# Threading attention through projections: logits first in a beat, another spread of the pieces, value differences later

## The chip, the cores and the metric

The kernel runs on one core of a Trainium2 chip. The metric is the device time of one execution in microseconds; the time before is the median of three runs. The core's engines are named as the profile names them: PE (matmuls and transposes), DVE (elementwise work, scans, reductions), ACT (activation functions, copies, scaling), POOL (masks, some transfers), SP (the queue of most transfers). PEld is PE's loading of weights into its array.

## The reference, cut to what matters

Two transformer blocks follow each other over 512 tokens of width 1024, in fp32.

```
h    = rmsnorm(concat(meta[16], x)) ; proj = h @ w_in
# block 1: eight "forgetting" heads beside a pooled path
s    = q.k / 8 + c[t] - c[s]   (causal; c is the running sum of log gates) ; p = softmax(s)
y    = (p @ v) * silu(z_attn)
x    = rmsnorm(x + merge(pooled path, y) @ w_out)
# block 2: eight heads with relative position bias, eight "stick-breaking" heads, MLP
p_ca = softmax(q.k / 8 + bias[rel], within chunks)
w_sb = exp(log_sigmoid(z) + suffix sum of log_sigmoid(-z))      (strictly causal)
x    = x + gt1 * (concat(w_sb @ v, p_ca @ v) @ w_o)
x    = x + gt2 * (relu(h2 @ w1)**2 @ w2)
```

Each head is 64 wide; queries are taken in four blocks of 128 rows.

## The kernel before

**Precision.** Every operand of a large product is kept as an upper part and a lower part of a rounded format (`hh` and `hl`, `wh` and `wl`, `ah` and `al`, `pth` and `ptl`), and a product is three matmuls (upper x upper, lower x upper, upper x lower; L1842 to L1844). The upper part is a copy on ACT, the lower a subtraction on DVE.

**Projections and steps.** The weights are cut into 76 units of 128 x 2048, loaded by SP into `raw`, copied to `wh` by ACT (L582) and subtracted to `wl` by DVE (L1081) in four parts of 128 x 512. Two such pairs exist, so a unit's parts are made while PE works on the unit before. PE walks through a unit in 16 steps of three matmuls with 512 columns each; the upper and lower parts of queries, keys and values that come out are made on ACT and DVE at fixed steps (L695, L706, L1228, L1239).

**Attention in pieces.** Attention is not a stage of its own. It is cut into pieces, and after each projection step PE issues as many pieces as a list of numbers says. `pieces_of` writes the row of pieces, `beats_of` spreads it. A piece is one of three:
- S h.i: the scores of head h, query block i, with keys 0 to i (L1988). Blocks go 3, 2, 1, 0.
- T h.j: transposes ("turns") of the probabilities of key block j, one for each query block from j on (L2009), into PSUM bank 3 or 6 in turn. A turn waits until DVE has emptied the bank of the turn before the last one.
- V h.j: values of key block j times the turned probabilities (L2038, L2041).

The row has the turns of head h and the scores of head h + 1 in alternation, then the values of head h. Heads 0 to 7 (called FG) run beside 160 steps of the first block, heads 8 to 15 (CA) and 16 to 23 (SB) beside 188 steps of the second. A place in the list is a beat; it holds one piece, or none if the head's queries and keys aren't ready at that step.

**The other engines** go through the same beats in the same steps, each task so many beats behind its piece (the table `AGE`). For an S on DVE: logits (L1253 with the row of sums, L1261 with the position bias) one beat behind, the maximum (L1268) two, the reciprocal (L1273) four, or, for heads 16 to 23, a scan (L1282) two. On ACT: the exponential (L714) three, the product with the reciprocal (L720, `norm`) five, or the sigmoid (L726) one. For a T: upper part on ACT one (`ph`, L739), lower part on DVE two (`pl`, L1293; the text calls its result ptl). For a head's last V: half of the output on ACT (L745), `both_out` on DVE (L1301), the gate (L1306), upper and lower part of the output (L754, L1311). Engines execute their instructions in the order written, so in a beat the order of tasks is the order in the queue.

**Value differences.** The value rows of the second block go to memory and come back shifted by one row (L523, L533). DVE subtracts them at the four steps in `DV` (L1576), ACT makes the upper part a step later (`DV_UPPER`, L974), DVE the lower part one step after that (`DV_LOWER`, L1580). The value pieces of heads 16 to 23 read them.

Of the kernel before, what the change touches and what calls it, by code (L numbers as in the profile page):

```python
# [55 lines left out]
FG, CA, SB = range(8), range(8, 16), range(16, 24)  # L56
# [13 lines left out]
def pieces_of(heads):  # L70

    out = []
    for n, h in enumerate([*heads, None]):
        scores = [] if h is None else [("S", h, i) for i in (3, 2, 1, 0)]
        if n:
            g = heads[n - 1]
            blocks = range(3, LAST_J[g] - 1, -1)
            for j in blocks:
                out.append(("T", g, j))
                if scores:  # L80
                    out.append(scores.pop(0))
            out += [("V", g, j) for j in blocks]
        for x in scores:
            out += [x] if n else [x, None]
    return out

AGE = dict(logits=1, max=2, exp=3, rcp=4, norm=5, sig=1, scan=2, ph=1, pl=2, half=1, both=2, oh=3, ol=4,
           gate=3, oh_fg=4, ol_fg=5)  # L90


def beats_of(pieces, per_step, ready):

    flat, first = [], []
    for g, n in enumerate(per_step):
        first.append(len(flat))
        for _ in range(n):
            flat.append(pieces.pop(0) if pieces and ready(pieces[0]) <= g else None)
    first.append(len(flat))  # L100
    return flat + pieces + [None] * 12, first


def program(nc, x, xcols, wall, wf, poolw, params, fng, wada, crow_in, rel, out):
# [30 lines left out]
    with ExitStack() as ctx:  # L135
        def sb(name, shape, dt=F32, where=ctx):
            return where.enter_context(nc.sbuf_tensor(name, shape, dt))
# [34 lines left out]
        half = sb("half", [128, 16])  # L172
# [111 lines left out]
        def raw_of(n, c):  # L284
# [2 lines left out]

        steps_f = 16 * 10
        f_qk = {p: m for m, (kind, p) in enumerate(ORDER_1) if kind == "qk"}
        beats_f, first_f = beats_of(pieces_of(FG), [0] * 16 + [1] * 112 + [1, 2] * 16,  # L290
                                    lambda x: 0 if x is None else 16 * (f_qk[x[1] // 2] + 1) + 7)

        steps_s = 188
        beats_s, first_s = beats_of(
            pieces_of(CA) + pieces_of(SB), [1, 1, 1, 1, 2] * 22 + [1, 1] + [1, 2] * 24 + [2] * 7 + [4] * 5 + [1] * 16,
            lambda x: 0 if x is None else 16 * (x[1] // 2 - 4) + 33 if x[1] in CA else 16 * (x[1] // 2 - 8 + 7) + 9 - 2 * (x[1] > 21))
        end_f, end_s = len(beats_f), len(beats_s)

# [70 lines left out]
        def ends(x):  # L369
            return x is not None and x[0] == "V" and x[2] == LAST_J[x[1]]  # L370
# [35 lines left out]
        TURN_BANK_2 = ((1, 0), (4, 5))  # L406
        VSB_OUT = (78, 79, 91, 95)

        DV, DV_UPPER, DV_LOWER = (87, 88, 104, 108), (88, 89, 105, 109), (89, 90, 106, 110)
        VSB_BANK, W_O_BANK = (0, 1, 2, 0), ((1, 0, 4, 5), (2, 3, 6, 7))  # L410

        def o_step(n):
# [159 lines left out]
        def _(e):  # L572
# [183 lines left out]
            def beat(flat, b_):  # L756
                def at(age):
                    return flat[b_ - age] if b_ >= age else None

                if (x_ := at(AGE["norm"])) and x_[0] == "S" and x_[1] not in SB:  # L760
                    normalize(*x_[1:])
                if ends(x_ := at(AGE["oh_fg"])) and x_[1] in FG and x_[1] % 2:
                    out_upper(x_[1])
                if ends(x_ := at(AGE["oh"])) and x_[1] not in FG and x_[1] % 2:
                    out_upper(x_[1])
                if (x_ := at(AGE["exp"])) and x_[0] == "S" and x_[1] not in SB:
                    exp(*x_[1:])
                if (x_ := at(AGE["sig"])) and x_[0] == "S" and x_[1] in SB:
                    sigmoid(*x_[1:])
                if (x_ := at(AGE["ph"])) and x_[0] == "T":  # L770
                    turned(*x_[1:])
# [305 lines left out]
        def _(e):  # L1077
# [236 lines left out]
            def beat(flat, b_):  # L1314
                def at(age):
                    return flat[b_ - age] if b_ >= age else None

                if ends(x_ := at(AGE["ol_fg"])) and x_[1] in FG and x_[1] % 2:
                    out_lower(x_[1])
                if ends(x_ := at(AGE["ol"])) and x_[1] not in FG and x_[1] % 2:  # L1320
                    out_lower(x_[1])
                if (x_ := at(AGE["rcp"])) and x_[0] == "S" and x_[1] not in SB:
                    inverse_sum(*x_[1:])
                if (x_ := at(AGE["scan"])) and x_[0] == "S" and x_[1] in SB:
                    sticks(*x_[1:])
                if ends(x_ := at(AGE["gate"])) and x_[1] in FG and x_[1] % 2:
                    out_gate(x_[1])
                if (x_ := at(AGE["max"])) and x_[0] == "S" and x_[1] in FG:
                    maximum(*x_[1:])
                if (x_ := at(AGE["pl"])) and x_[0] == "T":  # L1330
                    turned(*x_[1:])
                if ends(x_ := at(AGE["both"])):
                    both_out(x_[1])
                if (x_ := at(AGE["logits"])) and x_[0] == "S" and x_[1] not in SB:
                    logits(*x_[1:])


            e.wait_ge(a["v"], 5)
# [59 lines left out]
            for b_ in range(first_f[steps_f], end_f):  # L1398
                beat(beats_f, b_)
# [1010 lines left out]
```

## Time and profile before

| | |
|---|---|
| median of three runs | 1009.93 us (1009.12 to 1011.12) |
| profiled execution | 1012.43 us |
| its span | 1010.6 us |
| PE, PEld busy | 980.9 us (97%), 817.1 us (81%) |
| DVE, ACT busy | 657.3 us (65%), 485.5 us (48%) |

The profile is of one execution, whose time is a little above the median. The span is the time from the first to the last recorded instruction; 1.8 us of the execution's time lie outside it. Busy times are sums over an engine's instructions, and matmuls overlap, so a busy PE is not PE at its peak. A row of a timeline gives a start, a duration and, in brackets, how long the engine was idle before it and which instruction's end released it.

### The profile page before, as it was taken

Reading aid. Unit: us, or ns where it says so; the run is one execution under the profiler, and the core shown is the slowest. Engines: PE = TensorE matmul, PEld = TensorE weight load, DVE = VectorE, ACT = ScalarE, POOL = GpSimd, SP = SyncE. Lnnn points to the kernel's source line nnn. Section 1 sums busy time; section 2 is a strip of 40 time slices with the busy share of each in tenths; the row PEclk is TensorE's granted clock in tenths of the full one; section 3 lists DMA queues with packets and bytes.
Section 4 is the critical chain, followed back from the end, with each engine's and each line's share of the span. In section 5 each row is a group of like instructions: output and inputs, shape, how many; then the busy total and the mean of one; then the engine's idle time right before and its main releaser. Section 6 shows DMA issues by size and latency. Waiting matters only on the chain.

```text
span 1010.6 us, 13022 instructions
## 1 busy us (share of the span) xinstructions
PE 980.9 (97%) x4784; PEld 817.1 (81%) x4784; DVE 657.3 (65%) x1203; ACT 485.5 (48%) x963; POOL 70.5 (7%) x158
## 2 busy tenths in 40 slices
PE   8999999999999999999889999899999999999998
PEld 7888988788888888777778778788888888888886
DVE  6487878859787768467577776877444454445453
ACT  6458687743223445589685654334124223323420
POOL 4001001011112011000000000110000000000000
PEclk9999999999999999999999999999999999999999
DMA  7104221257789415342433225337413223322221
GB/s 294 75 25 178 67 103 53 84 197 291 286 289 331 174 56 153 114 125 78 136 94 115 63 63 207 127 103 131 163 56 112 84 86 123 107 102 84 84 73 52
DMA packets 34080, 129.81 MB, mean 128 GB/s; under 512 B 8905, under 2 KB 8905, under 8 KB 24418
## 3 DMA queue, kind: packets, MB, share of 16 engines
q1 hardware_dynamic: 23538, 98.27, 29.0%
q0 software_dynamic: 7408, 26.75, 7.6%
q10 hardware_dynamic: 3072, 3.98, 1.1%
q8 instruction: 38, 0.62, 0.3%
q14 instruction: 24, 0.20, 0.1%
HBM read 119.45 MB, written 5.27 MB: 123 GB/s over the span
## 4 chain that ended last, share of the span: by engine, by line
PE 78%; DVE 12%; ACT 4%; issue 3%; DMA 2%; SPq 0%; POOL 0%; ACTq 0%; DVEq 0%; POOLq 0%
PE psum L1842 23%; PE psum L1844 23%; PE psum L1843 23%; PE psum L2009 2%; DVE wl L1081 2%; PE psum L1988 2%; PE psum L2038 1%; PE psum L2041 1%; DMA raw<-in_wall 1%; DVE two L1620 1%; DVE ptl L1293 1%; DVE p_sb L1282 1%; DMA value_rows<-rows 1%; DVE hl L1121 1%; DVE tmp L1599 1%
## 5 line engine op out<-in xcount | busy, mean ns | idle before, releaser
L1842 PE MATMUL psum<-hh,wh 128*128 128x512 f32 (+1 forms) x720 | 277.2, 385 | 0.7 <-DVE hl L1121 0.6
L1844 PE MATMUL psum<-hh,wl 128*128 128x512 f32 (+1 forms) x720 | 268.5, 373 | 0.0
L1843 PE MATMUL psum<-hl,wh 128*128 128x512 f32 (+1 forms) x720 | 268.2, 373 | 0.0
L582 ACT ACTIVATE wh<-raw 128x512 fp32r<-128x512 f32 x292 | 169.5, 620 | 134.9 <-PE psum L1844 118.9
L1081 DVE TENSOR_TENSOR wl<-raw,wh 128x512 fp32r<-128x512 f32 x292 | 192.5, 684 | 18.1 <-ACT wh L582 17.6
L1844 PEld LDWEIGHTS psum<-hh,wl 128*128 128x128 f32 x720 | 135.6, 188 | 24.1
L1842 PEld LDWEIGHTS psum<-hh,wh 128*128 128x128 f32 x720 | 135.8, 189 | 22.8 <-DVE hl L1121 1.6
L1843 PEld LDWEIGHTS psum<-hl,wh 128*128 128x128 f32 x720 | 136.0, 189 | 19.1 <-issue 0.7
L1842 PE MATMUL psum<-wh,ah 128*128 128x512 f32 x320 | 125.8, 393 | 0.0
L1844 PE MATMUL psum<-wh,al 128*128 128x512 f32 x320 | 124.6, 389 | 0.0
L1843 PE MATMUL psum<-wl,ah 128*128 128x512 f32 x320 | 124.6, 389 | 0.0
L1599 DVE TENSOR_TENSOR tmp<-psum,gt 128x512 f32<-128x512 f32 x40 | 27.6, 690 | 86.3 <-PE psum L1844 85.5
L1844 PEld LDWEIGHTS psum<-wh,al 128*128 128x128 f32 x320 | 60.1, 188 | 12.6
L1842 PEld LDWEIGHTS psum<-wh,ah 128*128 128x128 f32 x320 | 60.1, 188 | 12.1 <-ACT p_sb L726 0.2
L1843 PEld LDWEIGHTS psum<-wl,ah 128*128 128x128 f32 x320 | 60.1, 188 | 11.7
L1682 DVE SCALAR_TENSOR_TENSOR sgt<-psum,two 128x512 f32<-128x512 f32 x32 | 22.1, 691 | 61.3 <-ACT two L1036 61.3
L2009 PE MATMUL psum<-ident,p_sb 128*128 128x128 f32 x272 | 48.5, 281 | 12.1 <-DVE ptl L1293 11.9
L1036 ACT ACTIVATE two<-psum 128x512 f32<-128x512 f32 x32 | 19.2, 600 | 78.4 <-PE psum L1844 78.4
L739 ACT ACTIVATE pth<-psum 128x128 fp32r<-128x128 f32 (+4 forms) x104 | 46.1, 445 | 21.8 <-PE psum L2009 21.1
L2009 PEld LDWEIGHTS psum<-ident,p_sb 128*128 128x128 f32 x272 | 34.7, 144 | 24.7 <-issue 16.2
L1293 DVE TENSOR_TENSOR ptl<-psum,pth 128x128 fp32r<-128x128 f32 (+1 forms) x96 | 46.2, 482 | 10.5 <-ACT pth L739 9.8
L714 ACT ACTIVATE p_sb<-p_sb,sm 128x528 f32<-128x528 f32 (+3 forms) x64 | 35.9, 561 | 8.6 <-DVE sm L1268 5.6
(282 smaller groups left out, 1468.0 us busy)
## 6 DMA issues: line engine op xcount, KB each, us to landing
raw<-in_wall SPq DMA_DIRECT2D x75, 1024.0 KB, 5.0
wa<-in_wada POOLq DMA_DIRECT2D x20, 512.0 KB, 5.9
gt<-in_wada POOLq DMA_DIRECT2D x20, 512.0 KB, 7.1
wb<-in_wada POOLq DMA_DIRECT2D x8, 512.0 KB, 7.3
xt<-in_xcols SPq DMA_DIRECT2D x8, 264.0 KB, 8.4
cb<-c_rows SPq DMA_DIRECT2D x8, 264.0 KB, 3.5
x<-in_x SPq DMA_DIRECT2D x4, 512.0 KB, 8.1
x_kept<-x SPq DMA_DIRECT2D x4, 512.0 KB, 2.8
```

Source lines behind the costliest of these rows:

```text
L582: e.activation(home(w)[0][:, 512 * c:512 * c + 512], raw_of(w, c), ACT.Copy).then_inc(a["wh"], 1)
L714: e.activation(block_p(h, i), block_p(h, i), ACT.Exp, bias=nmx, scale=1.0 if h in FG else -1.0, accum_out=su).then_inc(a["exp"], 1)
L739: e.activation(ph[0:rows, PT[j]:PT[j] + w_], bank[bk][0:rows, 0:w_], ACT.Copy).then_inc(a["turn"], 1)
L1081: e.tensor_tensor(home(w)[1][:, cs], raw_of(w, c), home(w)[0][:, cs].bitcast(F32), ALU.subtract).then_inc(v["wl"], 1)
L1293: e.tensor_tensor(dst, bank[bk][0:rows, 0:w_], ph[0:rows, o:o + w_].bitcast(F32), ALU.subtract).then_inc(v["turn"], 1)
L1599: e.tensor_tensor(dst, bank[bk], gt[:, j, 512 * ch:512 * ch + 512], ALU.mult).then_inc(sem, 1)
L1682: e.scalar_tensor_tensor(s2[n % 2], bank[w1_bank(n)], 0.0, two[:, n % 2, :], ALU.max, ALU.mult).then_inc(v["r2"], 1)
L1842: e.matmul(out_, lh, rh, start=start, stop=False, skip_group_check=True)
L1843: e.matmul(out_, lh, rl, start=False, stop=False, skip_group_check=True)
L1844: return e.matmul(out_, ll, rh, start=False, stop=stop, skip_group_check=True)
L1988: ins = e.matmul(dst[:, size * j:size * j + size], q[:, 128 * i:128 * i + 128], k[:, size * j:size * j + size], start=k is k_up, stop=k is ...
L2009: ins = e.transpose(bank[bk][:, 128 * (i - i0):128 * (i - i0) + 128], head(h)[0][:, o:o + 128], ident[:, :])
```

## The change

Four things are changed, and no instruction is added or taken away.

- `logits` is the first task of a DVE beat instead of the last.
- `AGE["norm"]` is 6 instead of 5.
- The numbers of pieces for each step come from two tables of digits, `PACE_F` and `PACE_S`, instead of regular lists. The old lists had one piece a step or a little more; the new ones have steps without a piece and steps with up to nine. Their sums are the same, 160 and 256.
- `DV`, `DV_UPPER` and `DV_LOWER` have the differences of row blocks 2 and 3 at steps 113 and 122 (and one and two steps later) instead of 104 and 108. Those of row blocks 0 and 1 stay at 87 and 88.

```diff
+PACE_F = [int(n) for n in ("00000000000000000011140110040102202010113010211101010115131000301121010101301202"
...
+PACE_S = [int(n) for n in ("11112111121111211112111121111211112002211200322014011101112010312102222120002304"
...
-AGE = dict(logits=1, max=2, exp=3, rcp=4, norm=5, sig=1, scan=2, ph=1, pl=2, half=1, both=2, oh=3, ol=4,
+AGE = dict(logits=1, max=2, exp=3, rcp=4, norm=6, sig=1, scan=2, ph=1, pl=2, half=1, both=2, oh=3, ol=4,
            gate=3, oh_fg=4, ol_fg=5)
...
-        beats_f, first_f = beats_of(pieces_of(FG), [0] * 16 + [1] * 112 + [1, 2] * 16,
+        beats_f, first_f = beats_of(pieces_of(FG), PACE_F,
...
-            pieces_of(CA) + pieces_of(SB), [1, 1, 1, 1, 2] * 22 + [1, 1] + [1, 2] * 24 + [2] * 7 + [4] * 5 + [1] * 16,
+            pieces_of(CA) + pieces_of(SB), PACE_S,
...
-        DV, DV_UPPER, DV_LOWER = (87, 88, 104, 108), (88, 89, 105, 109), (89, 90, 106, 110)
+        DV, DV_UPPER, DV_LOWER = (87, 88, 113, 122), (88, 89, 114, 123), (89, 90, 115, 124)
...
+                if (x_ := at(AGE["logits"])) and x_[0] == "S" and x_[1] not in SB:
+                    logits(*x_[1:])
                 if ends(x_ := at(AGE["ol_fg"])) and x_[1] in FG and x_[1] % 2:
                     out_lower(x_[1])
...
                 if ends(x_ := at(AGE["both"])):
                     both_out(x_[1])
-                if (x_ := at(AGE["logits"])) and x_[0] == "S" and x_[1] not in SB:
-                    logits(*x_[1:])
```

Line numbers of the changed kernel are 7 higher. The order of instructions at three places follows, first of the kernel before, then of the changed one.

DVE at the start of head 5 (p_sb is written by the logits, tmp 64x512 by both_out, tmp<-tmp,gt is the gate, ptl the turned lower part), before:

```order
L1301 TENSOR_TENSOR tmp<-psum,tmp 64x512
L1081 TENSOR_TENSOR wl<-raw,wh 128x512
L1228 SCALAR_TENSOR_TENSOR ah<-psum,ah 64x512 x2
L1306 TENSOR_TENSOR tmp<-tmp,gt 128x512
L1293 TENSOR_TENSOR ptl<-psum,pth 128x128
L1253 SCALAR_TENSOR_TENSOR p_sb<-psum,ccol,cb 128x528
```

The same place after:

```order
L1088 TENSOR_TENSOR wl<-raw,wh 128x512
L1235 SCALAR_TENSOR_TENSOR ah<-psum,ah 64x512 x2
L1308 TENSOR_TENSOR tmp<-psum,tmp 64x512
L1260 SCALAR_TENSOR_TENSOR p_sb<-psum,ccol,cb 128x528
L1313 TENSOR_TENSOR tmp<-tmp,gt 128x512
L1300 TENSOR_TENSOR ptl<-psum,pth 128x128
```

The logits of the head's first block have moved ahead of the gate and of the turned lower part.

DVE around the turns of head 14 and 15 (ptl2 is the turned lower part, sgt<-sgt,rows the difference of value row block 3, v_sb<-sgt,v_sb its lower part, x1<-x1,v_end the difference of row block 2, sm a reciprocal), before:

```order
L1273 RECIPROCAL sm<-sm 128x1
L1576 TENSOR_TENSOR sgt<-sgt,rows 128x512
L1081 TENSOR_TENSOR wl<-raw,wh 128x512
L1273 RECIPROCAL sm<-sm 128x1
L1301 TENSOR_TENSOR tmp<-psum,tmp 64x512
L1580 TENSOR_TENSOR v_sb<-sgt,v_sb 128x8x64
L1081 TENSOR_TENSOR wl<-raw,wh 128x512
L1293 TENSOR_TENSOR ptl2<-psum,pth2 128x128
L1293 TENSOR_TENSOR ptl2<-psum,pth2 128x256
L1293 TENSOR_TENSOR ptl2<-psum,pth2 128x384
```

The same place after:

```order
L1280 RECIPROCAL sm<-sm 128x1
L1088 TENSOR_TENSOR wl<-raw,wh 128x512 x2
L1308 TENSOR_TENSOR tmp<-psum,tmp 64x512
L1300 TENSOR_TENSOR ptl2<-psum,pth2 128x128
L1300 TENSOR_TENSOR ptl2<-psum,pth2 128x256
L1583 TENSOR_TENSOR x1<-x1,v_end 128x512
L1246 TENSOR_TENSOR low_2<-psum,k_sb2 64x512
L1300 TENSOR_TENSOR ptl2<-psum,pth2 128x384
```

The difference and its lower part have left the place ahead of the first ptl; that of row block 2, which stood earlier, now stands between the second ptl and the third.

DVE at head 18 (128x512 of p_sb2 is the scan of head 19's first block, low_2 a lower part of keys, al the output's lower part), before:

```order
L1301 TENSOR_TENSOR tmp<-psum,tmp 64x512
L1293 TENSOR_TENSOR ptl2<-psum,pth2 128x128
L1239 TENSOR_TENSOR low_2<-psum,k_sb2 64x512
L1311 TENSOR_TENSOR al<-tmp,ah 128x512
L1282 SCALAR_TENSOR_TENSOR p_sb2<-p_sb2,rows 128x512
L1239 TENSOR_TENSOR low_2<-psum,k_sb2 64x512
L1293 TENSOR_TENSOR ptl2<-psum,pth2 128x256
```

The same place after:

```order
L1246 TENSOR_TENSOR low_2<-psum,k_sb2 64x512 x2
L1308 TENSOR_TENSOR tmp<-psum,tmp 64x512
L1300 TENSOR_TENSOR ptl2<-psum,pth2 128x128
L1318 TENSOR_TENSOR al<-tmp,ah 128x512
L1289 SCALAR_TENSOR_TENSOR p_sb2<-p_sb2,rows 128x512
L1300 TENSOR_TENSOR ptl2<-psum,pth2 128x256
```

Both lower parts of keys stand ahead of the head's first ptl, and none is left between the scan and the second ptl.

## Rows read from the trace of the kernel before

**Rows 1.** The page's busy time, share of the span and instructions, by engine.

```profile
PE 980.9 (97%) x4784; PEld 817.1 (81%) x4784; DVE 657.3 (65%) x1203; ACT 485.5 (48%) x963; POOL 70.5 (7%) x158
```

**Rows 2.** Windows: length, then PE, PEld, DVE, ACT, POOL busy (x), PEclk, DMA, GB/s.

```profile
80.00:212.00 132.00, 127.09 (x804) 112.91 (x803) 106.37 (x219) 99.06 (x218) 13.26 (x33) 0.99 0.26 86
430.00:535.00 105.00, 95.09 (x464) 76.91 (x464) 69.76 (x187) 84.57 (x197) 2.80 (x12) 0.97 0.39 116
535.00:625.00 90.00, 85.80 (x464) 71.00 (x463) 67.57 (x111) 50.82 (x109) 2.19 (x4) 1.00 0.26 81
665.00:1010.60 345.60, 341.69 (x1527) 283.29 (x1526) 170.77 (x267) 103.78 (x184) 2.74 (x5) 1.00 0.31 99
```

**Rows 3.** Windows of 6 us behind PE's two longest waits.

```profile
504.00:510.00 6.00, 4.88 (x20) 4.34 (x21) 5.58 (x17) 5.57 (x14) 0.00 (x0) 0.72 0.20 45
528.00:534.00 6.00, 5.55 (x24) 4.78 (x25) 3.16 (x7) 2.83 (x5) 0.00 (x0) 0.72 0.73 223
```

**Rows 4.** PE's waits, 430 to 535: who waited <- for whom: total us, times, longest.

```profile
PE psum L2009 <- DVE ptl L1293: 6.1, 3, 2.6
PE psum L1988 <- DMA low<-low: 1.2, 1, 1.2
PE psum L1842 <- DVE wl L1081: 1.1, 1, 1.1
PE psum L1842 <- DVE qk L1557: 0.8, 1, 0.8
PE psum L2271 <- ACT two L959: 0.6, 1, 0.6
```

**Rows 5.** PE's waits, 535 to 625.

```profile
PE psum L2009 <- DVE ptl L1293: 3.9, 4, 1.3
PE psum L2038 <- DVE ptl L1293: 0.2, 1, 0.2
```

**Rows 6.** PE's timeline, heads 0 to 7: start, us, instruction, [idle before <- releaser].

```profile
94.28 0.64 PE L1988 MATMUL psum<-k_sb,ah 128*128 128x400 f32 x2 [1.30 <-DVE p_sb L1253]
...
154.57 0.63 PE L1988 MATMUL psum<-k_sb,ah 128*128 128x400 f32 x2 [1.57 <-DVE p_sb L1253]
...
200.24 0.93 PE L2009 MATMUL psum<-ident,p_sb 128*128 128x128 f32 x4 [1.93 <-DVE ptl L1293]
```

**Rows 7.** DVE's timeline, value differences of row block 0, then 3.

```profile
499.25 0.69 DVE L1576 TENSOR_TENSOR x<-x,rows 128x512 f32<-128x512 f32 x1 [3.61 <-DMA x<-value_rows]
...
523.78 0.67 DVE L1576 TENSOR_TENSOR sgt<-sgt,rows 128x512 f32<-128x512 f32 x1
...
526.82 0.67 DVE L1580 TENSOR_TENSOR v_sb<-sgt,v_sb 128x512 fp32r<-128x512 f32 x1
```

**Rows 8.** DVE's timeline at head 18.

```profile
568.12 1.21 DVE L1282 TENSOR_TENSOR_SCAN p_sb<-p_sb,rows 128x512 f32<-128x512 f32 x1
569.35 0.69 DVE L1239 TENSOR_TENSOR low<-psum,k_sb 64x512 fp32r<-64x512 f32 x1
570.08 0.43 DVE L1293 TENSOR_TENSOR ptl<-psum,pth 128x256 fp32r<-128x256 f32 x1
```

**Rows 9.** DVE's timeline at the start of head 5.

```profile
152.83 0.69 DVE L1306 TENSOR_TENSOR tmp<-tmp,gt 128x512 f32<-128x512 f32 x1
153.55 0.29 DVE L1293 TENSOR_TENSOR ptl<-psum,pth 128x128 fp32r<-128x128 f32 x1
153.76 0.76 DVE L1253 SCALAR_TENSOR_TENSOR p_sb<-psum,ccol,cb 128x528 f32<-128x528 f32 x1
```

**Rows 10.** PE's timeline, turns of heads 13, 15 and 18, and a score.

```profile
505.12 0.71 PE L2009 MATMUL psum<-ident,p_sb 128*128 128x128 f32 x3 [2.63 <-DVE ptl L1293]
...
528.45 0.52 PE L2009 MATMUL psum<-ident,p_sb 128*128 128x128 f32 x3 [2.58 <-DVE ptl L1293]
...
565.80 0.63 PE L1988 MATMUL psum<-v_ca 128*128 128x512 f32 x2
...
570.65 0.52 PE L2009 MATMUL psum<-ident,p_sb 128*128 128x128 f32 x3 [0.97 <-DVE ptl L1293]
```

More of the change, by code:

```diff
@@ L85, in pieces_of @@
     return out
-AGE = dict(logits=1, max=2, exp=3, rcp=4, norm=5, sig=1, scan=2, ph=1, pl=2, half=1, both=2, oh=3, ol=4,
+PACE_F = [int(n) for n in ("00000000000000000011140110040102202010113010211101010115131000301121010101301202"
+                           "02000112030230300100300103023301100000110301311112112203021301123113200500330023")]
+PACE_S = [int(n) for n in ("11112111121111211112111121111211112002211200322014011101112010312102222120002304"
+                           "10211203011201010231200160011001211203331201110233120022213230100115031020203441"
+                           "3020305539041021021210001211")]
+AGE = dict(logits=1, max=2, exp=3, rcp=4, norm=6, sig=1, scan=2, ph=1, pl=2, half=1, both=2, oh=3, ol=4,
            gate=3, oh_fg=4, ol_fg=5)
```

## The prediction, on record before the result

> **What bounds the kernel now.** I read the page's busy line first. PE is busy 980.9 of 1010.6 us [rows 1], so about 30 us can be won on TensorE at all, and DVE and ACT matter only where PE waits for them. The windows then say where those 30 us lie. The change touches only the stretches in which attention is threaded through projections: 80 to 212 us (heads 0 to 7), 430 to 535 (heads 8 to 15) and 535 to 625 (heads 16 to 23). PE is idle there 132.00 − 127.09 = 4.9, 105.00 − 95.09 = 9.9 and 90.00 − 85.80 = 4.2 us, 19.0 together [rows 2].
>
> A long wait costs a second time. Over the three stretches the granted clock reads 0.99, 0.97 and 1.00 [rows 2], but it reads 0.72 in the 6 us from 504 and in the 6 us from 528 [rows 3], just behind the two longest waits: 6 × (1 − 0.72) = 1.7 us of lost work each, in which PE still reads busy. The ceiling is 19.0 + 3.4 = 22.4 us.
>
> The Trainium skill ("Perfetto Trace Analysis", Identifying the Most-Contended Engine) says that the busy share of matmuls is a poor measure, since they are pipelined, and that the weight loads' share is a good one. The trace agrees at the low clock, where PE reads 5.55 of 6 us busy [rows 3]. By that rule 430 to 535 (76.91 of 105 us) would lose 105 × (1 − 0.732 / 0.820) = 11.3 us against the undisturbed end of the program (283.29 of 345.60) [rows 2], where idle time gives 9.9. My sum would be about a seventh larger by it, which lies inside its uncertainty.
>
> Who ends the waits? In 430 to 535 three waits for the lower part of turned probabilities (DVE L1293) make 6.1 us; the rest is a DMA of keys 1.2, a weight's lower half 1.1, a normalised query 0.8, and squares from ACT 0.6 [rows 4]. In 535 to 625 it is L1293 again, 3.9 in four waits [rows 5]. In the first stretch the three longest are two waits for logits (1.30, 1.57) and one for L1293 (1.93) [rows 6]. L1293 itself is short, 0.29 to 0.43 us [rows 8, 9]: what is late is what stands ahead of it in DVE's and ACT's queues.
>
> **Part one, logits first.** DVE does the same instructions in another order. At head 5's start the gated product (0.69) and a ptl (0.29) stand ahead of the logits at 153.76 [rows 9], for which PE waits 1.57 at 154.57 [rows 6]. In the new order they stand behind, so the logits end 0.98 earlier, and PE comes to the waiting score one projection step later. A step is three matmuls, and where nothing disturbs them 1527 take 345.60 us [rows 2], 0.23 each: a step is 0.70. 0.98 + 0.70 covers 1.57: **+1.6**. The wait of 1.30 at 94.28 is of the same kind, but there a weight's lower half comes to stand ahead of the logits: I take half, **+0.7** (0 to 1.3). The price of logits first is that each ptl of the beat waits one logits (0.76 [rows 9]) more. In the old order the beat before had put the same logits ahead of it, so this shows only at the first turned block of a head, and nobody waits for that one alone.
>
> **Part two, normalising a beat later.** The product on ACT goes one beat behind, so ACT's queue no longer stops for a reciprocal just made. Who waits for it is the turn that reads it. In the order of pieces ten or more stand between a score and that turn, against an age of six: no cost, and if a bunch eats the cover, a product (under 0.76, the logits' time for the same block [rows 9]). The exceptions are heads 0 and 8, where six stand. At T8.0 the product and a turned upper part share a beat on an ACT that is busy 84.57 of 105 us [rows 2]: I take a new wait of 0.9 (0 to 1.3), charged below.
>
> **Part three, the spread of pieces.** The totals are the same, so PE's own work is. SP's queue moves one load of a head's row of sums past one load of a weight unit, POOL's keeps its order; no wait of PE is for either load [rows 4 to 6], so both cost 0. What changes is which wait falls where.
> - 200.24 (1.93 [rows 6]) moves to the next turn, a quarter of a step on: **+0.3**.
> - 430 to 500: the DMA wait of 1.2 stays, since the first score of head 8 waits for its keys, ahead of all pieces. The other four (6.1 less the two of 2.63 and 2.58 leaves 0.9; then 0.6, 0.8, 1.1) [rows 4, 10] are 3.4; steps with no piece come to stand ahead of three of them. I leave 0.5 and charge T8.0's 0.9: 3.4 − 0.5 − 0.9 = **+2.0** (0 to 3.4).
> - T13.1 at 505.12 (2.63 [rows 10]): DVE had stood 3.61 us for rows of values coming back by DMA [rows 7]. Neither that subtraction's step nor the transfer moves. PE now arrives two steps (1.40) sooner, and DVE has a logits (about 0.67) ahead of the ptl where it had a lower half of values and one of weights, 2 × 0.67 by the form at 526.82 [rows 7], so 0.67 less. 2.63 + 1.40 − 0.67 = 3.4, and ACT's copy of values stands behind more: wait 3.6, **−1.0** (0 to −2.7). Its low clock stays.
> - The two longest of 535 to 625, 0.97 at 570.65 (head 18's last turn) [rows 10] and 1.3 (head 20's) [rows 5]: ahead of the ptl that the first waits for, DVE does a scan (1.21), then a lower half of keys (0.69) [rows 8]. In the new order both lower halves of keys (1.38) come before the scan, where DVE waits anyway. That is more than the step (0.70) by which the distance on PE shrinks. **+1.0** and **+1.3**. The other two waits of the stretch stay: 0. The 0.2 for a value piece [rows 5] goes, **+0.2**.
>
> **Part four, value differences later.** The difference of row block 3 (0.67) and its lower half (0.67) stand on DVE at 523.78 and 526.82 [rows 7], ahead of the ptl for which PE waits 2.58 at 528.45 [rows 10]. They go to steps 122 and 124, with ACT's copy between them; those of row block 2 come to steps 113 and 115, behind the second ptl of the head, where no wait is. They move past lower halves of weights and keys and head 15's pieces; their readers are the value pieces of head 16, over ten steps behind, so they cost nothing there (without that cover, 0.67 each). With 1.34 less on DVE about 0.6 of the wait is left: 2.0. With a wait that short the clock should not fall, since it did not behind 0.97 and 1.3 (1.00 over 535 to 625 [rows 2, 5]): 1.7. **+3.7**.
>
> **New waits.** Bunches are new. In step 104 six pieces stand together, and the third (T14.0) takes over a PSUM bank whose ptl stands behind a logits: 0.67 + 0.43 on DVE against about 0.6 for two pieces on PE, so 0.5. In step 147 five pieces stand together, with a scan of 1.21 [rows 8] ahead of a ptl. No row prices these; the nearest are the short waits of [rows 4, 5], 0.2 to 1.1. I take five places at 0.56, nearest to the one worked out: **−2.8** (0 to −6).
>
> Sum: 1.6 + 0.7 + 0.3 + 2.0 − 1.0 + 1.0 + 1.3 + 0.2 + 3.7 = 9.8; less 2.8 is 7.0. The profiled execution took 1012.43 us (span 1010.6 and 1.8 around it), 0.25% above the median of the runs: 1005.4 is 0.69% less, so 1009.93 becomes **1003.0**.
>
> **Rivals.**
> - *Smaller gain.* ACT, 81% busy in 430 to 535 [rows 2], sets the pace: part three's +2.0 is 0, T13.1 costs 2.0 rather than 1.0, and the terms of 535 to 625 are halved (−1.2). 9.8 − 4.2 − 2.8 = 2.8, median 1007.1. Against it: of the waits of [rows 4] one is named for ACT, 0.6.
> - *Slower: the latency stays.* From the score at 565.80 to the turn at 570.65 pass 4.85 us [rows 10]. If the chain of sigmoid, scan and both turned parts takes that whatever stands beside it, a bunch only takes a step (0.70) out of PE's distance, and each joint between heads pays: heads 16 to 19 two steps at four joints, 5.6; heads 8 to 13 one step at five, 3.5; head 15 one, 0.7; 9.8 together. Of the gains are left 1.6 + 0.7 + 0.3 + 1.0 (half of +2.0) + 0.2 + 1.7 (the clock at 528) = 5.5. Net 4.3 slower, median 1014.2. It decides where DVE has less than 0.7 us of movable work ahead of the ptl. Against it: at 569.35 such work, 0.69, is seen inside the chain [rows 8].
> - *Everything on L1293 and the logits goes*: 1.3 + 1.57 + 1.93 + 6.1 + 3.9 + 0.2 = 15.0, and one low clock, 1.7: 16.7, median 993.3. The 3.61 us for value rows speak against it.
> - *No change:* the new waits are as large as the 9.8, median 1009.9. That the pieces don't move at all is excluded by the order of instructions.
>
> **How the numbers follow.** Forecast 0.48 (its own range 1000 to 1006), smaller gain 0.25, slower 0.14, all gone 0.07, no change 0.06. A measurement can tell about 0.2%, 2.0 us, from no change: faster is below 1007.9, slower above 1011.9. The smaller gain lies a third of the time within the bound: faster 0.48 + 0.17 + 0.07 = 0.72, same 0.08 + 0.06 = 0.14, slower 0.14. The range 997.5 to 1010.0 leaves out the slower case and most of the one in which all goes.
>
> **What would show it.** Right: the wait of head 5's score gone; no wait over 1 us near 528 and a clock of 1.00 there; PE idle in 535 to 625 near 2; DVE still waiting 3 to 4 us for value rows, with a PE wait of about 3.6 and a low clock behind it. Wrong: waits for L1293 of over 1 us inside the bunches of steps 104 and 147, or a clock of 0.72 at a place that had none; then the allowance is what failed.

## The result, and the profile after

The changed kernel takes 994.56 us (median of four runs, 993.92 to 996.30) against 1009.60 of the kernel before: a ratio of 0.985, with a 95% interval of 0.9836 to 0.9863. The prediction had 1003.0 and a range from 997.5 to 1010.0. The direction was right, the gain was twice what was forecast, and the time lies below the range.

The profiled execution of the changed kernel has a span of 992.8 us, 17.8 less than the 1010.6 of before. The medians differ by 15.0: the execution that was profiled before was one of the slower ones. The page's busy line (engine, busy us, share, instructions), to be read against [rows 1]:

```profile
PE 974.2 (98%) x4784; PEld 813.3 (82%) x4784; DVE 656.1 (66%) x1203; ACT 483.6 (49%) x963; POOL 69.9 (7%) x158
```

The same instructions, and DVE and ACT as busy as before. PE's busy time fell by 6.7 us although its work is the same.

To see where 17.8 us went, a stage has to be cut at the same matmul in both kernels, not at the same time. I cut at the first matmuls of five weight units: heads 0 to 7 run from 75.21 to 216.71 before and from 74.90 to 211.75 after; heads 8 to 15 from 418.74 to 534.90 and from 413.82 to 520.22; heads 16 to 23 from 534.90 to 656.24 and from 520.22 to 638.45. Outside these the two differ by 0.3 us. Windows of the kernel before, cut so (columns as in [rows 2]):

```profile
75.21:216.71 141.50, 136.47 (x851) 120.76 (x849) 114.27 (x232) 105.06 (x228) 14.76 (x36) 0.99 0.28 92
418.74:534.90 116.16, 106.25 (x510) 85.26 (x508) 76.50 (x197) 91.74 (x210) 2.80 (x12) 0.97 0.39 116
534.90:656.24 121.34, 114.41 (x601) 94.47 (x600) 96.24 (x167) 63.94 (x138) 4.81 (x10) 1.00 0.32 110
```

And of the changed kernel:

```profile
74.90:211.75 136.85, 134.49 (x851) 119.29 (x849) 111.50 (x229) 103.04 (x226) 12.62 (x33) 1.00 0.28 94
413.82:520.22 106.40, 101.86 (x507) 81.94 (x506) 74.48 (x195) 90.44 (x209) 2.80 (x12) 1.00 0.42 127
520.22:638.45 118.23, 113.96 (x603) 94.87 (x603) 98.03 (x171) 64.11 (x139) 4.82 (x10) 1.00 0.33 113
```

The stages are 4.65, 9.76 and 3.11 us shorter. The second column gives PE's idle time as length less busy: 5.0, 9.9 and 6.9 before, 2.4, 4.5 and 4.3 after, so 10.7 us of idle time went. The seventh column is the granted clock: 0.99 and 0.97 became 1.00. Before, there were three falls of the clock in these stages (near 200, 505 and 528 us), after there is none. A window of 6 us around one reads 0.72; windows of 3.4 us inside each (columns as above) show what a fall is:

```profile
201.50:204.90 3.40, 3.40 (x13) 2.74 (x12) 3.37 (x6) 1.90 (x4) 0.00 (x0) 0.50 0.00 0
505.30:508.70 3.40, 3.40 (x14) 3.02 (x13) 3.26 (x11) 2.97 (x8) 0.00 (x0) 0.50 0.34 77
529.20:532.60 3.40, 3.40 (x13) 2.82 (x13) 1.70 (x3) 2.63 (x5) 0.00 (x0) 0.50 0.84 291
```

For 3.4 us the clock is 0.50 (1.2 GHz, the lower of its two levels) and then 1.00 again, which costs half of 3.4, 1.7 us; three falls are 5.1 us. What is left, 17.5 − 10.7 − 5.1 = 1.7 us, is neither idle time nor clock; it comes up again below.

PE's waits in the stage of heads 8 to 15 after, to be read against [rows 4] (who waited <- for whom: total us, times, longest):

```profile
PE psum L2016 <- DVE ptl L1300: 2.7, 2, 2.2
PE psum L1849 <- DVE wl L1088: 1.2, 2, 0.7
PE psum L1995 <- DMA low<-low: 0.5, 1, 0.5
```

The 6.1 us in three waits for the turned lower part are 2.7 in two, and the waits for a query and for squares are gone.

### The profile page after: what moved, and what is told of

Its sections match the earlier page's. It is cut to its first block, busy times and chain, and to the rows that moved or that the text cites. A ratio compares the mean times of both kernels' runs of the same rounds, so it can differ in the third digit from the quotient of the medians.

```text
span 992.8 us, 13022 instructions
## 1 busy us (share of the span) xinstructions
PE 974.2 (98%) x4784; PEld 813.3 (82%) x4784; DVE 656.1 (66%) x1203; ACT 483.6 (49%) x963; POOL 69.9 (7%) x158
## 4 chain that ended last, share of the span: by engine, by line
PE 82%; DVE 9%; ACT 4%; issue 2%; DMA 2%; POOL 0%; SPq 0%; DVEq 0%; ACTq 0%; POOLq 0%
PE psum L1849 24%; PE psum L1851 24%; PE psum L1850 24%; PE psum L2016 2%; PE psum L1995 2%; PE psum L2045 1%; PE psum L2048 1%; DVE wl L1088 1%; DVE two L1627 1%; PE psum L1883 1%; DVE hl L1128 1%; DMA value_rows<-rows 1%; ACT wh L589 1%; DVE two L1492 1%; DMA raw<-in_wall 1%
## 5 line engine op out<-in xcount | busy, mean ns | idle before, releaser
L1849 PE MATMUL psum<-hh,wh 128*128 128x512 f32 (+1 forms) x720 | 274.0, 381 | 0.7 <-DVE hl L1128 0.6
```

Source lines behind the costliest of these rows:

```text
L1849: e.matmul(out_, lh, rh, start=start, stop=False, skip_group_check=True)
```

## The experiments

Each kernel is timed against the kernel before on the same chip. The table at the end of this section gives the three stages of each from its profile. Two theories stood against each other. Theory A: the new spread of the pieces brings most. Theory B: the order of tasks within DVE's and ACT's queues brings most.

**Logits first alone** moves the two lines of `logits` to the head of a DVE beat:

```diff
+                if (x_ := at(AGE["logits"])) and x_[0] == "S" and x_[1] not in SB:
+                    logits(*x_[1:])
                 if ends(x_ := at(AGE["ol_fg"])) and x_[1] in FG and x_[1] % 2:
                     out_lower(x_[1])
...
-                if (x_ := at(AGE["logits"])) and x_[0] == "S" and x_[1] not in SB:
-                    logits(*x_[1:])
```

> The kernel before with logits first in each DVE beat and nothing else. Theory A (the spread of pieces brings most of the 15 us): only the two waits for logits in heads 0 to 7 get shorter (1.57 and 1.30), 1 to 2.5 us faster, nothing in heads 8 to 23. Theory B (the order within DVE's and ACT's queues brings most): about 5 us faster, with the waits for L1293 in heads 8 to 15 shorter too. On record my prediction had +1.6 for head 5 alone.

Measured: a ratio of 0.9999 (0.9987 to 1.0011), no change. The two waits for logits shrank from 2.9 us to 1.3, and the stage of heads 0 to 7 lost 1.2 us of idle time. But heads 8 to 15 gave it back: T13.1 waited 3.65 us instead of 2.63, and T10.1 1.42 instead of 0.85; the stage has 0.6 us more idle time. Part of the 1.0 at T13.1 is the new order: its ptl now stands behind a logits of 0.68, and from the first value difference to that ptl pass 5.71 us instead of 5.45. The larger part is that PE stood at the turn 2.5 us after the value rows were there, and not 3.2. Why that distance shrank is not shown. Both theories had expected a gain.

**The product one beat later alone** (`norm=5` to `norm=6`):

> The kernel before with ACT's product with the reciprocal one beat later and nothing else. Theory A: within 1 us of before. Theory B: ACT no longer stops for reciprocals, about 3 us faster, most of it between 430 and 535 us.

Measured: 0.9959 (0.9941 to 0.9977), 4 us faster. PE's waits between 418 and 530 us in its profile:

```profile
PE psum L2016 <- DVE ptl L1300: 3.9, 3, 1.8
PE psum L1849 <- DVE wl L1088: 1.1, 1, 1.1
PE psum L1849 <- DVE qk L1564: 0.8, 1, 0.8
PE psum L1995 <- DMA low<-low: 0.5, 1, 0.5
```

The 6.1 of [rows 4] are 3.9, the wait for squares from ACT is gone, and of two falls of the clock one is left. That is theory B's number, for this part. ACT, the busiest engine behind PE in this stage, had been stopping for reciprocals, and turned upper parts and squares were queued behind. Its waits for them in this stage, before and in this kernel:

```profile
ACT p_sb L720 <- DVE sm L1273: 4.4, 9, 0.9
ACT p_sb L727 <- DVE sm L1280: 0.6, 2, 0.4
```

**Value differences later alone** (steps 113 and 122 for blocks 2 and 3):

```diff
-        DV, DV_UPPER, DV_LOWER = (87, 88, 104, 108), (88, 89, 105, 109), (89, 90, 106, 110)
+        DV, DV_UPPER, DV_LOWER = (87, 88, 113, 122), (88, 89, 114, 123), (89, 90, 115, 124)
```

> The kernel before with the differences of value row blocks 2 and 3 at steps 113 and 122 and nothing else. Both theories: the wait of 2.58 us at 528 falls to 0.6 and the low clock of 1.7 us behind it goes, 3 to 4 us faster; the wait at T13.1 (2.63) and its low clock stay. If the low clock does not hang on that wait, 2 us.

Measured: 0.9984 (0.9968 to 1.0001), too small to be clear of no change. In the profile the mechanism is as expected: T15.1's wait fell from 2.58 to 0.76 us, and the low clock behind it went, 3.5 us together. But in the next stage a new wait of 0.61 stands at 543.9, and that stage is 1.2 us longer. The differences are not free at steps 122 to 124: the wait of about 0.6 is in all three profiles with the regular spread and the differences late. The 1.2 is not all theirs, since the kernel before has 122.12 instead of 121.34 in a second profile.

**The spread alone** (both tables, nothing else):

```diff
-        beats_f, first_f = beats_of(pieces_of(FG), [0] * 16 + [1] * 112 + [1, 2] * 16,
+        beats_f, first_f = beats_of(pieces_of(FG), PACE_F,
...
-            pieces_of(CA) + pieces_of(SB), [1, 1, 1, 1, 2] * 22 + [1, 1] + [1, 2] * 24 + [2] * 7 + [4] * 5 + [1] * 16,
+            pieces_of(CA) + pieces_of(SB), PACE_S,
```

> The kernel before with both tables of the spread and nothing else. Theory A: 9 to 12 us faster. Theory B: the spread was made for the other order of tasks and alone brings 0 to 3 us, with waits for logits inside the bunches of over 1 us each.

Measured: 998.78 us, 0.9889 (0.9868 to 0.991), 11.4 us faster: theory A. All three stages are shorter, by 3.2, 7.7 and 3.1 us. Its waits between 415 and 524:

```profile
PE psum L2016 <- DVE ptl L1300: 2.8, 2, 2.6
PE psum L1849 <- DVE wl L1088: 1.1, 2, 0.6
PE psum L1849 <- DVE qk L1564: 0.6, 1, 0.6
PE psum L1995 <- DMA low<-low: 0.5, 1, 0.5
```

The long one is T15.1's, 2.61 us at 518, with a low clock behind it; the value differences are still at steps 104 and 108 here.

**The changed kernel less one part.** Four kernels take one part back each, with the diffs above reversed.

> The changed kernel with logits last in each DVE beat again. Theory A: 1 to 3 us slower than the changed kernel (about 996.5). Theory B: 6 us or more slower (over 1000.5), with PE waits for logits in the bunches.

> The changed kernel with ACT's product at age 5 again. Theory A: within 1 us of the changed kernel, T8.0's wait a little shorter. Theory B: 3 us or more slower, between 430 and 520 us.

> The changed kernel with the value differences of row blocks 2 and 3 at steps 104 and 108 again. They then stand in and behind the bunch of six pieces at step 104. If the value differences were what held T15.1: 3 to 4 us slower with a clock of 0.72 near 516 us. If the spread has already moved T15.1 away from them: within 1 us.

> The changed kernel with the regular spread of before (so logits first, product later and value differences later, together). Theory A: 9 to 11 us slower than the changed kernel, near 1004. Theory B: 3 us slower at most, near 997.

Measured, with the changed kernel at 994.56 us (ratio 0.985):
- logits last: 997.04, 0.9871 (0.9857 to 0.9886). Logits first is worth 2.5 us here (2.1 by the two ratios), where alone it was worth nothing. The difference between the two profiles is mostly in heads 0 to 7 (139.01 against 136.85): waits for logits of 1.0 us come back instead of 0.2, idle time grows by 1.1 us in all, and another 1.1 is neither idle time nor clock.
- product at age 5: 994.07, 0.984 (0.9824 to 0.9856). The part that alone brought 4 us brings nothing beside the others. ACT does stop for reciprocals again, 2.8 us in nine waits in this stage, but with the new spread nobody on PE's path stands behind it.
- value differences early: 997.22, 0.9881 (0.9864 to 0.9897), 2.7 us slower. T15.1's wait is back, without a fall behind it in this profile:

```profile
517.71 0.52 PE L2016 MATMUL psum<-ident,p_sb 128*128 128x128 f32 x3 [2.21 <-DVE ptl L1300]
```

- the old spread: 1006.18, 0.9963 (0.9951 to 0.9974). The three other parts together bring 3.7 us, the spread on top of them 11.6. Theory A, but its 9 to 11 was a little low.

**What holds T13.1.** The prediction said that this wait would grow, because DVE stands for value rows that come back by DMA. In the changed kernel it is 2.19 us. DVE's rows ahead of it, then PE's row:

```profile
490.48 0.69 DVE L1583 TENSOR_TENSOR x<-x,rows 128x512 f32<-128x512 f32 x1 [3.64 <-DMA x<-value_rows]
491.99 0.69 DVE L1583 TENSOR_TENSOR x<-x,rows 128x512 f32<-128x512 f32 x1 [0.81 <-DMA x<-value_rows]
```

```profile
494.82 0.41 PE L2016 MATMUL psum<-ident,p_sb 128*128 128x128 f32 x2 [2.19 <-DVE ptl L1300]
```

DVE's wait of 3.64 is that of [rows 7]. ACT's upper part of the same turn was ready at 492.96, 1.4 us before DVE came to the ptl at 494.40, so ACT doesn't set this turn:

```profile
492.68 0.28 ACT L746 ACTIVATE pth<-psum 128x128 fp32r<-128x128 f32 x1
```

Two kernels put the differences of row blocks 0 and 1 at steps 91 and 93, behind T13.1's tasks, one with the product at age 6 and one at 5:

```diff
-        DV, DV_UPPER, DV_LOWER = (87, 88, 113, 122), (88, 89, 114, 123), (89, 90, 115, 124)
+        DV, DV_UPPER, DV_LOWER = (91, 93, 113, 122), (92, 94, 114, 123), (93, 95, 115, 124)
```

> The changed kernel with the differences of value row blocks 0 and 1 also later, at steps 91 and 93 instead of 87 and 88, behind T13.1 in DVE's order. Theory V (DVE stands for the value rows' transfer, and T13.1 waits for that): the wait of 2.19 us at T13.1 goes, none takes its place, 2 us faster than the changed kernel, near 992.5. Theory W (the turned upper part on ACT sets T13.1): the wait stays within 0.5 us of 2.19 and the time too.

> As the last one, with ACT's product at age 5 as before. If the later product has no worth with the new spread: the same time as the last one, within 0.1%. If it costs something: 1 us faster than it.

Measured: 993.04 (0.9841, 0.981 to 0.9872) and 993.50 (0.9846, 0.9815 to 0.9877). Theory V: the 2.19 is gone. But a wait took part of its place, so the gain was 1.5 us and not 2; with age 6:

```profile
PE psum L1849 <- DVE wl L1088: 1.2, 2, 0.7
PE psum L2045 <- DVE ptl L1300: 0.7, 1, 0.7
PE psum L2016 <- DVE ptl L1300: 0.5, 1, 0.5
PE psum L1995 <- DMA low<-low: 0.5, 1, 0.5
```

The 0.7 at L2045 is a value piece behind block 1's instructions. The age of the product makes no difference that can be told, as before.

**Is the spread needed for the long waits?** The kernel before, with its regular spread and logits last, with age 6 and all four differences late (91, 93, 113, 122):

> The kernel before, regular spread and logits last, with the product one beat later and all four value differences later (91, 93, 113, 122). If the two long waits of heads 13 and 15 hang on the value differences alone, both go with both low clocks, with what the later product brings: about 8 us faster than before, near 1002. If the new spread is needed for them: 1005 or more.

Measured: 1003.32 us, 0.9938 (0.9921 to 0.9955), 6.3 us faster where about 8 was expected. Its stage of heads 8 to 15 is 106.69 us, only 0.3 longer than the changed kernel's 106.40:

```profile
PE psum L1849 <- DVE wl L1088: 1.2, 1, 1.2
PE psum L2016 <- DVE ptl L1300: 1.1, 2, 0.6
PE psum L1849 <- DVE qk L1564: 0.8, 1, 0.8
PE psum L1995 <- DMA low<-low: 0.5, 1, 0.5
```

So in this stage there were two ways to nearly the same gain: to move what stood ahead of two ptl's, or to move PE's pieces. The gains don't add: this kernel is 9.5 us shorter here than the one before, the spread alone 7.7, both together (with logits first, differences at 91 and 93) 11.1. They overlap in T13.1's wait and its fall, which the profile with the spread alone doesn't have either (2.6 + 1.7), in the wait for squares (0.6) and in the DMA wait (1.15 to 0.5 in both). T15.1's wait goes with the value differences only; the spread alone leaves it at 2.61. In the stages of heads 0 to 7 and 16 to 23 this kernel is no shorter than the one before (141.29 against 141.50, 122.72 against 121.34); there the spread is what helps.

**Keys between scan and ptl.** The prediction's +1.0 and +1.3 rested on the lower halves of keys that stand on DVE between a scan and a ptl [rows 8]. This kernel is the one before with those halves two steps later for two groups:

```diff
-                    SB_LOWER.setdefault(n_ + (9 if p_ == 3 and sub_ else 10), []).append((p_, sub_, part_))
+                    SB_LOWER.setdefault(n_ + (11 if p_ == 3 and sub_ else 12 if p_ == 2 and sub_ else 10), []).append((p_, sub_, part_))
```

> The kernel before with the lower halves of head pair 20's and 22's keys two steps later on DVE (148 and 149, 163 and 164 instead of 146, 147 and 161, 162), so that none stands between the scan and the turned lower part. My prediction's theory: the waits of 0.97 at T18.0 and 1.34 at T20.0 go, 2.0 to 2.3 us faster. Rival (the chain of sigmoid and scan sets them, as in the slower case of the prediction): both waits stay above 0.7.

Measured: 1.0036 (1.0019 to 1.0053), 3.6 us slower, and yet the theory holds for the waits. T18.0's 0.97 is gone (0.43 is left at a value piece), T20.0's 1.34 is 0.47. What was missed is the other reader of those instructions. The halves read the PSUM bank into which the next projection writes, and PE came there first (v_ca is here the buffer in which the keys lie):

```profile
593.12 0.78 PE L1842 MATMUL psum<-wh,ah 128*128 128x512 f32 x1 [2.93 <-DVE v_ca L1239]
```

```profile
592.00:598.00 6.00, 4.88 (x19) 4.26 (x20) 2.64 (x5) 0.00 (x0) 0.00 (x0) 0.72 0.19 44
```

A wait of 2.93 us and 1.7 us of low clock, where 1.4 were won (0.97 + 1.34, less the 0.43 and 0.47 that are left). The changed kernel leaves the keys where they are and moves the pieces.

**Does a fall of the clock belong to a wait or to an execution?** Three kernels were profiled a second time: the changed kernel, the one before, and logits first alone.

> The changed kernel, profiled a second time. If a fall of the clock belongs to a wait: again none behind the wait of about 2.2 us at T13.1 near 495, and the stages as long as before to 0.3 us, but for the value rows' transfer. If it belongs to the execution: a clock of 0.72 for 6 us in one place, 1.7 us more.

> The kernel before, profiled a second time. If a fall belongs to a wait: the same three, behind 200, 505 and 528 us, 5.1 us. If to the execution: another number or other places.

> The kernel before with logits first alone, profiled a second time. The same wait of 1.93 us near 200: with a low clock behind it this time if the execution decides, without one if the kernel does.

Both, as it came out. The changed kernel again has no fall (stages 136.67, 106.30, 118.33). The kernel before again has the two in heads 8 to 15, but not the one near 200, although the wait is the same. The window behind the wait in the first execution (its row stands in [rows 6]), then the row of the wait and the window in the second:

```profile
200.00:206.00 6.00, 5.65 (x25) 4.68 (x26) 5.45 (x10) 3.12 (x7) 0.00 (x0) 0.72 0.00 0
```

```profile
200.10 1.14 PE L2009 MATMUL psum<-ident,p_sb 128*128 128x128 f32 x6 [1.93 <-DVE ptl L1293]
```

```profile
200.00:206.00 6.00, 5.80 (x32) 4.56 (x32) 5.36 (x9) 2.99 (x7) 0.00 (x0) 1.00 0.00 0
```

Logits first alone had no fall near 200 in either. Over all profiles with that wait of 1.93 us, six had the fall and three had not. Of eleven waits of 2.48 to 3.94 us in heads 13 and 15 ten had a fall right behind them; the eleventh, 2.83 us in the first profile of logits first, had none, and the fall behind the wait before it lasted twice as long. No wait under 1.7 us in the three stages had one.

**The last wait of that kind.** The changed kernel with block 0's difference at step 91 and block 1's at 98:

```diff
-        DV, DV_UPPER, DV_LOWER = (87, 88, 113, 122), (88, 89, 114, 123), (89, 90, 115, 124)
+        DV, DV_UPPER, DV_LOWER = (91, 98, 113, 122), (92, 99, 114, 123), (93, 100, 115, 124)
```

> The changed kernel with the value difference of row block 0 at step 91 and that of block 1 at step 98. Theory V: the wait of 0.72 at 500 in the run with 91 and 93 was for a ptl behind block 1's instructions and goes, 0.7 us faster than that run, near 992.3. Rival: that wait is for the bunch of value pieces itself and stays; then the same time.

Measured: 992.70 us (992.40 to 992.88), 0.9822 (0.9801 to 0.9843), the fastest version. The wait of 0.7 at L2045 is 0.2:

```profile
PE psum L1849 <- DVE wl L1088: 1.2, 2, 0.7
PE psum L1995 <- DMA low<-low: 0.5, 1, 0.5
PE psum L2016 <- DVE ptl L1300: 0.5, 1, 0.5
PE psum L2045 <- DVE ptl L1300: 0.2, 1, 0.2
```

In the trace the stage is 104.66 us against 105.10; by the medians, 0.34 us between two sessions on two chips, the two kernels can't be told apart. Against the changed kernel its runs lie 1.9 us lower and don't overlap (the highest is 992.88, the lowest of the changed kernel 993.92).

**All stages.** Length in us of the stage, PE's idle time in it, and the number of falls of the clock in it, from one profile each (the two of logits first in its first profile are one of 6.8 us):

```
kernel                              heads 0-7        heads 8-15       heads 16-23
before                              141.50  5.0  1   116.16  9.9  2   121.34  6.9  0
before again                        139.84  5.1  0   115.28  9.1  2   122.12  7.3  0
changed                             136.85  2.4  0   106.40  4.5  0   118.23  4.3  0
changed again                       136.67  2.2  0   106.30  4.4  0   118.33  4.3  0
before + logits first               138.99  3.9  0   115.98 10.5  2   121.40  7.0  0
before + logits first, again        139.16  3.9  0   116.98 10.9  2   121.41  7.0  0
before + product later              141.32  5.1  1   111.46  6.7  1   121.14  6.7  0
before + values later               141.50  5.1  1   111.93  7.4  1   122.56  7.5  0
before + spread                     138.34  3.4  0   108.51  5.1  1   118.22  4.2  0
changed, logits last                139.01  3.5  0   107.24  5.1  0   118.30  4.3  0
changed, product at 5               136.50  2.3  0   104.37  2.6  0   118.29  4.3  0
changed, values early               136.68  2.2  0   107.57  5.7  0   118.18  4.2  0
changed, old spread                 140.82  4.2  1   111.11  6.7  1   122.23  7.4  0
changed, rows 0, 1 at 91, 93        136.66  2.2  0   105.10  3.1  0   118.33  4.3  0
  the same, product at 5            136.51  2.4  0   105.44  3.2  0   118.31  4.3  0
before + product, all rows later    141.29  5.0  1   106.69  3.9  0   122.72  7.6  0
before, keys later                  141.41  5.1  1   115.88  9.9  2   125.91  9.1  1
changed, rows 0, 1 at 91, 98        136.72  2.2  0   104.66  2.6  0   118.36  4.3  0
```

A single profile carries some luck. With the product at 5 the changed kernel's stage of heads 8 to 15 is 2.0 us shorter than the changed kernel's own, but the medians are the same to 0.5 us: in that execution the value rows came early (DVE waited 0.62 for them, not 3.64), and T13.1 did not wait at all. The age may have a part in that: the other profile with the new spread, the product at 5 and rows 0 and 1 early (the spread alone) has a wait of 1.09 for the rows and none at T13.1, while the four with the product at 6 have 3.2 to 4.1 and 1.65 to 2.33. No run separates the two, and the medians leave 0.5 us for it at most.

## Why the prediction was wrong, step by step

- **The ceiling** of 22.4 us was sound and counted two of the three falls. About 14 of it was won (10.7 of idle time and 3.4 of clock), and 1.7 for the third fall besides. The share of the weight loads, with which I checked it, was no check: it doesn't show the low clock. In the three stretches at 0.50 above it is 2.74 to 3.02 of 3.40 us, 0.81 to 0.89, against 0.82 where nothing disturbs.
- **New waits, −2.8: the first of the two terms that failed.** It was put in without a row that priced it. The changed kernel has no wait inside either bunch that I named. In step 104 I had put two pieces of PE's time (0.6 us) against 0.67 + 0.43 of DVE's. The trace shows the score S15.2 at 506.47, then a whole projection step, and only then the bunch:

```profile
507.02 0.56 DVE L1268 CUSTOM_DVE_ANT_0 p_sb<-psum,sgt 128x384 f32<-128x384 f32 x1 [0.56 <-PE psum L1995]
...
507.50 0.42 DVE L1300 TENSOR_TENSOR ptl<-psum,pth 128x256 fp32r<-128x256 f32 x1
```

```profile
506.47 0.34 PE L1995 MATMUL psum<-ah 128*128 128x384 f32 x1
...
508.08 0.62 PE L2016 MATMUL psum<-ident,p_sb 128*128 128x128 f32 x4
```

  The ptl ends at 507.92 and T14.0 starts at 508.08 without a wait. I had left out that pieces are issued after their own step's three matmuls (0.70). In step 147 the five pieces found everything ready too. T8.0, for which I had charged 0.9, waited 0.09. Small new waits did come elsewhere, 0.45 at 155.43, 0.33 at 533.20 and two of 0.2 (89.72, 588.22), 1.2 us together. They are inside the sums by stage below, where the other gains were as much larger than said.
- **T13.1, −1.0: the second term that failed, wrong in sign and worth 3.1 us.** DVE did stand 3.6 us for value rows, as I said. But the wait was 2.19 us, 0.4 shorter and not 1.0 longer, and it had no low clock behind it, which I had said would stay (1.7). PE did come earlier, by 1.1 us against the transfer (1.40 was said): the transfer was issued at 487.77 instead of 496.57, 8.8 us sooner, and PE stood at the turn at 492.63 instead of 502.49, 9.9 sooner. The mis-sized term is DVE's: from the first difference to the ptl it took 3.92 us (490.48 to 494.40) instead of 5.45 (499.25 to 504.70), 1.5 less where I had 0.67. 2.63 + 1.1 − 1.5 is the 2.2 that was measured; the 0.2 for ACT's copy of values was not seen.
- **T15.1, +3.7: right.** With value differences later alone the same place gave 1.8 + 1.7 = 3.5, and 0.5 us of wait is left in the changed kernel (0.6 was said). That they cost nothing elsewhere was wrong with the old spread (0.61 at 543.9) and right to 0.1 us with the new one: there is a wait of 0.33 at 533.20, but with the differences early one of 0.24 stands a little later, and the stage is as long (118.23 and 118.18).
- **The other waits of heads 8 to 15, +2.0:** 3.4 us in four waits became 1.2 in two, +2.2. The DMA wait that "stays" went from 1.15 to 0.51: 0.6 more. It is 0.49 to 0.54 in all twelve profiles that have the new spread or the product at 6, and 0.75 to 1.25 in the six that have neither, so it follows the edits; only its size before is the execution's.
- **Heads 0 to 7, 1.6 + 0.7 + 0.3:** 2.7 us of idle time went, as summed. But that the low clock at 200 stays was wrong: 1.7. The wait of 1.93 is now two, 0.68 and 0.65, and neither has a fall behind it. That logits first makes nobody wait was wrong too: in the profile with it alone T13.1 waited 1.0 us more, 0.3 of it by DVE's queue.
- **Heads 16 to 23, 1.0 + 1.3 + 0.2:** 2.7 of idle time against 2.5, right, and the mechanism of the lower halves of keys is shown by the kernel that moved only those.
- **The product a beat later, 0:** right in the changed kernel, where taking it back changes nothing, and wrong alone, where it is worth 4 us. I had looked for who waits for the product, and not for who is queued behind the instruction that waits for the reciprocal.
- **The rivals.** The slower one, in which the latencies stay and the spread takes distance from PE, did not happen in any stage. The one in which everything goes (993.3, chance 0.07) has nearly the size that was measured, but not for its reason: 5.1 of the 17.5 us are clock, not waits, where it had counted one fall, and of the waits for ptl and logits 6.2 of 15.0 are left. My objection to it, the 3.61 us for value rows, was true and didn't count for much: that wait of DVE cost PE 2.2 us and no clock. The smaller gain, in which ACT sets the pace, didn't come either: with the new spread even an ACT that stops for reciprocals costs no time.
- **The signs.** Of those for being right five came (the score of head 5, T15.1, the clock there, the idle time of 535 to 625 with 1.5 us for the 2 said, DVE's wait for value rows); the wait of 3.6 with a low clock behind it didn't. The two signs for being wrong didn't come either: I had looked only for a gain that is too small.

In sum: 2.8 for new waits that didn't come, 3.1 at T13.1, 1.7 for the fall near 200, 0.6 at the DMA wait and 1.7 that no term had make 9.9 of the 10.5 us between forecast (7.0) and profiles (17.5 in the three stages). So the two steps that failed are an allowance for bunches and DVE's time ahead of T13.1's ptl; what the runs show is bunches without a wait and 2.19 us instead of 3.6, with no fall behind it. Why there is no fall stays open.

## What to carry to other kernels

When an engine that sets the end is interleaved with work of others, cut the trace at the same instruction in both kernels, and look at what stands ahead of the awaited instruction in its queue, and at who else is queued behind any instruction that itself waits. To move the consumer's pieces can be worth more than to reorder the producers: the keys moved on DVE won two waits and lost more at the next projection. Two changes that clear the same wait are worth it once, so a part's worth measured alone (0 for logits first, 4 us for the product) may be nothing like its worth beside the others (2 to 2.5 us and 0).

## What the runs showed of the hardware

**Falls of the clock come with some executions of a wait and not with others.** A wait of 1.93 us at the same instruction had 6 us at 0.72 behind it in six profiles and none in three, two of these profiles being of the same kernel. It is 3.4 us at 0.50 and costs 1.7 us each time. The Trainium skill ("TensorE: Matmul & The Clock Gate", Part 1) calls the clock's slow phase at a kernel's start variable from run to run, since what watches TensorE runs freely; the traces show a variation in mid-kernel too, and don't show its reason. The kernel before with two or three such waits spread from 1005.49 to 1013.49 us over its runs, the changed kernel from 993.92 to 996.30, and the last version, with no wait over 0.8 us in these three stages but those before the MLP (1.2 and 1.3), from 992.40 to 992.88. The falls make most of that scatter. With every run stands its mean granted clock, and over the 63 runs of the kernel before in the experiments it goes from 0.994 to 1.000: two runs at 1.000 took 1006.18 and 1006.29 us, the 21 at 0.995 took 1011.70 in the median. Time and lost clock (time × (1 − clock)) go together with a slope of 1.1 us per us and a correlation of 0.90. The median run of the kernel before lost 4.0 us so, the four of the changed kernel 0 to 2.0. Of the 15.0 us between the medians the clock is thus about 3.5, by this estimate, and not the 5.1 of the profiled pair. With the new spread waits of 2.06, 2.19 and 2.33 us at T13.1 and of 2.21 at T15.1 had no fall, one of 2.61 there had one; with the old one waits of 1.79, 2.17 and 2.26 us at T13.1 had one. Why stays open.

**The same matmuls take 1.7 us less.** Length less idle time and low clock is 134.8, 102.8 and 114.4 us in the three stages before and 134.5, 101.9 and 114.0 after. With the spread alone heads 8 to 15 have 101.8, with everything but the spread 102.7, so in that stage it comes with the spread. The first matmul of a step there has a mean of 432 ns before and 420 after, without those beside a fall or a wait. PE goes from steps to pieces or back 164 times in that stage before and 114 times after. Fewer changes are a possible cause, but in heads 0 to 7 they fall from 216 to 136 and only 0.3 us goes; no run isolates it.
